# Moving the normalisation of a block into the next round, the masks ahead of the variance, and the key turns behind half a step

## What is computed

```
S_t = S_{t-1} diag(w_t) - (S_{t-1} kk_t)(kk_t*a_t)^T + v_t k_t^T ;  y_t = S_t r_t
mean = mean(y); var = mean(square(y - mean))          # over the 64 columns of a head
yn = (y - mean) * rsqrt(var + GN_EPS)
out = (yn * gn_w + gn_b + bonus) * g
```

## Time and profile before

| | |
|---|---|
| median of three runs | 1400.87 us (1399.13 to 1403.6) |
| profiled execution, its own time | 1397.37 us |
| span in that profile | 1395.7 us |
| PE busy | 1304.2 us, 93% |
| DVE / ACT / POOL busy | 635.5 / 470.3 / 250.8 us |
| the four rounds | about 192 to 355 us of the span |
| behind them to the second half of the output product | 355 to 386 us |

### The profile page before, as it was taken

How to read it: one execution, slowest core, us unless ns; L and a number is a source line. 1 busy time by engine, 2 the same in 40 slices (tenths; PEclk the granted TensorE clock), 3 DMA queues, 4 the chain that set the end, 5 groups by cost and what they waited for, 6 DMA issues and landing times.

```text
span 1395.7 us, 25137 instructions
## 1 busy us (share of the span) xinstructions
PE 1304.2 (93%) x10577; PEld 1163.4 (83%) x10577; DVE 635.5 (46%) x763; ACT 470.3 (34%) x758; POOL 250.8 (18%) x228
## 2 busy tenths in 40 slices
PE   5999989888799999999999887987999999999998
PEld 5677878777699889988899876865998899988998
DVE  5578635454347552134422646265255432245323
ACT  4446435335245222222222431266232211222222
POOL 6013325232102220012211030110003200022000
PEclk9999999999899999999999998998999999999999
DMA  5223100001052322223242122100313322222321
GB/s 181 75 61 120 61 2 3 2 3 50 14 182 75 107 91 95 90 91 104 72 151 92 61 68 91 61 1 19 118 61 104 106 91 91 90 90 90 106 92 61
DMA packets 99929, 108.95 MB, mean 78 GB/s; under 512 B 1907, under 2 KB 97189, under 8 KB 99845
## 3 DMA queue, kind: packets, MB, share of 16 engines
q1 hardware_dynamic: 99764, 107.45, 23.9%
q0 software_dynamic: 80, 0.26, 0.1%
HBM read 105.60 MB, written 2.10 MB: 77 GB/s over the span
## 4 chain that ended last, share of the span: by engine, by line
PE 78%; DVE 9%; issue 5%; ACT 4%; POOL 2%; DVEq 2%; POOLq 1%; ACTq 0%; DMA 0%
PE ps L404 11%; PE ps L406 11%; PE ps L405 11%; PE ps L439 10%; PE ps L440 10%; PE ps L441 10%; DVE w_lo L1420 2%; PE ps L490 1%; PE ps L491 1%; PE ps L492 1%; PE ps L432 1%; PE ps L430 1%; PE ps L431 1%; DVE rcnt L1911 1%; PE ps L668 1%
## 5 line engine op out<-in xcount | busy, mean ns | idle before, releaser
L1420 DVE TENSOR_TENSOR w_lo<-w_raw,w_hi 128x2048 fp32r<-128x2048 f32 (+1 forms) x93 | 212.1, 2280 | 241.4 <-ACT w_hi L985 238.2
L439 PE MATMUL ps<-w_hi,a_hi 128*128 128x256 f32 x1024 | 288.4, 282 | 0.9 <-DVE w_lo L1420 0.9
L440 PE MATMUL ps<-w_lo,a_hi 128*128 128x256 f32 x1024 | 288.0, 281 | 0.0
L441 PE MATMUL ps<-w_hi,a_lo 128*128 128x256 f32 x1024 | 288.0, 281 | 0.0
L404 PE MATMUL ps<-h_hi,w_hi 128*128 128x512 f32 x672 | 270.9, 403 | 13.1 <-DVE w_lo L1420 12.8
L406 PE MATMUL ps<-h_hi,w_lo 128*128 128x512 f32 x672 | 266.1, 396 | 0.0
L405 PE MATMUL ps<-h_lo,w_hi 128*128 128x512 f32 x672 | 266.0, 396 | 0.0
L985 ACT ACTIVATE w_hi<-w_raw 128x2048 fp32r<-128x2048 f32 (+1 forms) x90 | 171.2, 1903 | 162.8 <-PE ps L441 141.1
L2141 POOL TENSOR_TENSOR hsq<-tmp 128x512 f32<-128x512 f32 x64 | 103.3, 1616 | 568.3 <-ACT tmp L989 568.3
L439 PEld LDWEIGHTS ps<-w_hi,a_hi 128*128 128x128 f32 x1024 | 193.2, 189 | 1.5 <-DVE w_lo L1420 1.3
L440 PEld LDWEIGHTS ps<-w_lo,a_hi 128*128 128x128 f32 x1024 | 193.2, 189 | 0.2
(11 more groups left out here) (316 smaller groups left out, 1845.8 us busy)
## 6 DMA issues: line engine op xcount, KB each, us to landing
w_raw<-w_ffn_up_dram SPq DMA_DIRECT2D x16, 1024.0 KB, 5.3
w_raw<-w_ffn_down_dram SPq DMA_DIRECT2D x16, 1024.0 KB, 5.0
w_raw<-w_up_dram SPq DMA_DIRECT2D x16, 1024.0 KB, 5.3
w_raw<-w_down_dram SPq DMA_DIRECT2D x16, 1024.0 KB, 4.9
w_raw<-w_in_first_dram SPq DMA_DIRECT2D x12, 1024.0 KB, 5.3
w_raw<-w_out_dram SPq DMA_DIRECT2D x8, 1024.0 KB, 5.9
w_raw<-w_in_dram SPq DMA_DIRECT2D x8, 1024.0 KB, 5.3
xn<-x_dram SPq DMA_DIRECT2D x8, 512.0 KB, 6.5
```

The source lines that it names most:

```text
L439: mm(o, hi[:, hb + k, tok], whi, start=first and own and k == ks[0], stop=False, skip_group_check=True)
L440: mm(o, hi[:, hb + k, tok], wlo, start=False, stop=False, skip_group_check=True)
L441: m = mm(o, lo[:, hb + k, tok], whi, start=False, stop=last and k == ks[-1], skip_group_check=True)
L1420: v.tensor_tensor(w_lo[:, g % 2, :, 0:n], w_raw[:, g % 2, :, 0:n], w_hi[:, g % 2, :, 0:n].bitcast(F32), ALU.subtract).then_inc(sm["w_lo_re ...
```

## The change

- PE: `turn_keys(i)` leaves `beside(i, 9)` and comes behind the second `attend` of the last step, still with its waits for `v_ready` and `kap_ready` (in the last round for `yc_ready` alone). The last round's `turn_output(2)` goes to bank 7, and `out_part(3)`, which writes bank 7, gets a wait for `y_scaled`.
- ACT: `turned_keys(i)` (the two evacuations) comes behind the second `attend` too. The squares carry a scale of 64^-0.5. Behind the last block's outputs ACT takes the square root of its variance.
- DVE: `variance(i-1)` moves from n = 7, where it stood before the masks of LA, to n = 8, behind them and before the masks of KA. `normalised(i-1)` leaves n = 8 and comes at n = 1 of the next round (as `normalised(i-2)`); only in the last round it stays at n = 8. For the last block DVE takes the reciprocal of ACT's root. The variance's second instruction only adds.
- POOL: `root` of the last block is gone.

```diff
@@ PE, beside(i, n)
                 if n == 9 and i + 1 < NB:
                     pe.wait_ge(sm["ka_masked"], 2 * i + 4)
                     turn_values(i + 1)
-                    pe.wait_ge(sm["v_ready"], i + 2)
-                    pe.wait_ge(sm["kap_ready"], i + 2)
-                    turn_keys(i)
                 if n == 9 and i + 1 == NB:
-                    pe.wait_ge(sm["yc_ready"], i)
-                    turn_output(i - 1, 2)
-                    pe.wait_ge(sm["y_scaled"], i)
-                    turn_keys(i)
+                    turn_output(i - 1, 7)
@@ PE, rounds
                     attend(m + 1)
+                if i + 1 < NB:
+                    pe.wait_ge(sm["v_ready"], i + 2)
+                    pe.wait_ge(sm["kap_ready"], i + 2)
+                else:
+                    pe.wait_ge(sm["yc_ready"], i)
+                turn_keys(i)
@@ PE, behind the rounds
             out_part(2, 0, HP)
+            pe.wait_ge(sm["y_scaled"], NB - 1)
             out_part(3, 0, HP)
@@ ACT
-                af(ysq[:, :, :], yc[:, :, :], ACT.Square).then_inc(sm["ysq_ready"], 1)
+                af(ysq[:, :, :], yc[:, :, :], ACT.Square, scale=N ** -0.5).then_inc(sm["ysq_ready"], 1)
...
-                if n == 9:
-                    turned_keys(i)
...
+                turned_keys(i)
...
             output(NB - 1, 2)
+            act.wait_ge(sm["var_ready"], NB)
+            af(yrs[:, :], var[:, :], ACT.Sqrt).then_inc(sm["yrs_ready"], 1)
@@ DVE
-                v.tensor_scalar(var[:, :], var[:, :], 1.0 / N, GN_EPS, ALU.mult, ALU.add).then_inc(sm["var_ready"], 1)
+                v.tensor_scalar(var[:, :], var[:, :], GN_EPS, None, ALU.add).then_inc(sm["var_ready"], 1)
...
                 dve.wait_ge(sm["yrs_ready"], i + 1)
+                if i + 1 == NB:
+                    v.reciprocal(yrs[:, :], yrs[:, :])
+                    dve.drain()
...
-                if n == 7 and i:
-                    variance(i - 1)
+                if n == 1 and i > 1:
+                    normalised(i - 2)
                 if n == 7 and i + 1 < NB:
                     masked(i + 1, LA, "la_done", "la_masked")
                 if n == 8 and i:
+                    variance(i - 1)
+                if n == 8 and i + 1 == NB:
                     normalised(i - 1)
...
                 if n == 9 and i + 1 == NB:
-                    scaled_output(i - 1, 2)
+                    scaled_output(i - 1, 7)
@@ POOL, behind the rounds
             shifted_output(NB - 2)
-            root(NB - 1)
             shifted_output(NB - 1)
```

## The result

The changed kernel took 1380.65 us (median of four runs, 1380.14 to 1381.18) against 1400.82 (1399.13 to 1403.6) for the kernel before: ratio 0.986, interval 0.9843 to 0.9878. Over all jobs of this study (67 timed runs of the kernel before, median 1399.6, 1397.0 to 1405.0; 13 of the changed one, median 1381.2, 1380.1 to 1383.3) it is 18.5 us. The 67 leave out x1's twelve runs of the kernel before, which would not move their median by more than 0.1. Executions that lie far off are left out of every figure here: two of the kernel before of 1842 us at a mean granted clock of 0.65, one of 4454 us in x2 and one of 6408 us in x4. The two profiled executions took 1397.37 and 1380.14 us: 17.2 apart.

A forecast was written before the change was run, and what follows sets the result against it. The rounds were taken as bound by PE's order, with DVE's program, waiting for POOL's root, releasing their ends. Gains 7.55 + 4.1 + 0.3 + 1.6 = 13.55, say 13.5 us, off 1400.87 gave 1387.4 us; range 1382 to 1393.5.

The forecast's parts named there:

- turn 1 to 2: Passage from round 1 to 2: scores 0.8, PE's gap 3.5, clock 2.4, key turns 0.85; 7.55 us won.
- the clock's 2.4: Turn from round 1 to 2: half clock behind PE's gap goes, 2.4 us won, bounds 0 to 3.4.
- the key turns' 1.65: Key turns behind the second attend no longer wait for ACT's copies: 0.3, 0.85 and 0.5 us in the three turns.
- turn 2 to 3: Passage from round 2 to 3: scores 0.8, gap 2.77, keys 0.5; 4.1 us won, bounds 3 to 4.5.
- the tail's root: Last block's root moves from POOL to ACT; multiply some 0.9 us earlier but hidden by out_part(3), gain 0.
- the last solve's start: Last round: key turns directly follow turn_output, no longer waiting for bank 2; 1.6 us won, bounds 0.5 and 4.5.
- rival B: Last round gets its clock back, key turns and solve faster: 15.8 us won, 1385.1 us; chance 0.12.
- so I take the difference off the median: Whole kernel: profiled execution lies 3.5 us below the median, so the 13.5 us come off 1400.87, giving 1387.4.
- A: Rounds: the half clock only moves elsewhere, so the 2.4 is not won: 11.1 us won, 1389.8; chance 0.15.
- C: Turns: ACT becomes the bound, key copies behind a waiting exponential; 2.2 us lost, 11.3 won, 1389.6; chance 0.13.
- D: Half clock from the last round's larger gap lasts up to 380 us: 18 us more, 1405.4, slower; chance 0.03.
- E: Rounds: POOL keeps masks or first levels late, the 3.5 gap stays; about 5 us won, 1395.9; chance 0.05.

The follow-up runs named there:

- x1: The kernel before, unchanged, profiled and timed again: 1399.75 us median, single runs 1397.56 to 1403.76.
- x2: The kernel before with only the key turns and their ACT evacuations moved behind each round's second attend: 1399.41 us against 1399.04, ratio 0.9998.
- x4: The changed kernel with the last round's part undone (turn_output through bank 2, key turns behind y_scaled): 1388.29 us.
- x6: The changed kernel with twelve small DVE multiplies ahead of the masks of KA in round 1, putting a gap back: 1392.02 us.
- x3: The kernel before with only DVE's two moves in the rounds (variance, normalising): 1388.98 us, ratio 0.9922.
- x8: The changed kernel with the last block's root back on POOL, without DVE's reciprocal: 1381.26 us, ratio 0.9871.
- x5: The kernel before with 14 extra PE matmuls ahead of the last round's turn_output(2): 1398.22 us against 1400.45, ratio 0.9978.
- x9: The changed kernel itself, profiled and timed again: 1382.96 us (1381.98 to 1383.25).
- x13: The changed kernel with 22 extra PE matmuls behind the last turn of the output: 1381.73 us.
- x14: The changed kernel with x13's 22 fillers and block 2's output turned only behind the last solve: 1380.75 us.
- x15: The changed kernel with nine extra PE matmuls (2.05 us) behind the last solve: 1385.07 us.
- x16: The changed kernel with 18 extra PE matmuls (4.1 us) behind the last solve: 1386.61 us.

## Why the prediction was wrong

**Right.** What bound the rounds (DVE's wait for the root, handed on to PE at their ends); turn 1 to 2 with its four terms (7.75 against 7.55: 4.4 against 4.3 for scores and gap, 3.4 against 3.25 for clock and keys), the clock's 2.4 among them (2.3 by x6); the key turns' 1.65 in all, in the stage once the gaps are gone (1.7 in x4 against x3), though not in the total time (0.7 there, nothing in x2); turn 2 to 3 (4.6 against 4.1: the first double follows the keys at once, and `key_values` waited for no copy); turn 0 to 1 (0.3); the moved multiply at nothing (0.65 us under DVE's wait for the next half copy); the tail's root at nothing (x8); the last solve's start (2.1 against 1.6: the key turns at full clock took 0.9 less, and the inverse, named as late next, then bound it).

**Wrong, first step.** "The solve itself stays at the half clock: 3.68 us". It took 1.96. The forecast took the larger gap before `turn_output` as the reason for the half clock and gave the other outcome (rival B) 0.12. x4 has the gap and, behind it, the wait of 2.9 us, and falls to half clock; the changed kernel has the same gap without that wait, and doesn't; x5 fills both and doesn't. The solve took 3.3 to 3.7 us in all five profiles with bank 2 and no filler (the kernel before, x1 to x4), and 1.96 or 1.97 in x5 and in all fourteen with the edit. So it is the edit in the last round that gave the solve its clock back: 2.0 us in the two profiles behind the start of the solve, 2.7 between x4 and the changed kernel. Why x6 had half clock for the turns just ahead of the solve, and the other profiles with the edit had not, stays open.

**Wrong, second step.** "so I take the difference off the median". That holds only if both medians lie as far above their profiled executions, and they lay 3.5 and 0.5 us above them. Of the 20.2 us, 2.9 are this; over all jobs, with medians of 1399.6 and 1381.2, the difference of 18.5 is only 1.3 above that of the profiles. That the change took away stretches which the first profile lacked is not shown: by x1 those lie at the entry of round 0 and behind the stage, where nothing was changed, and x9 has the first of them in the changed kernel too. So most of the 2.9 is the luck of which executions four runs drew. The range took 2 us for scatter and held it to be the same on both sides. With x9's job (1382.96) the result would have been inside; so it would with either of the two steps put right by itself (2.0 or 2.9 us on 1380.65, against the range's 1382).

**The rivals.** A (the half clock only moves) fails in the rounds and is seen elsewhere: x2, x13 and x14. B came. C: the exponential does stand before the key copies, and nothing waited for them. D and E did not come; in no profile did the half clock last from the last round to the last turn of the output.

**Open.** Where half clock falls in the stages behind 380 us, and why it is stable within most jobs and differs between them. The experiments ran on five chips, one for each job, so a difference between chips is a rival that no run here excludes; x9's three slower runs and its faster one, on one chip, show that it can't be all of it. x15 and x16 don't decide whether it depends on the time of arrival.

## What to carry to other kernels

A root computed by another engine should not stand in front of masks that the critical engine waits for: issue the multiply one round later, where its engine waits anyhow. When TensorE's waits are removed at several places, count the half clock behind each and ask what is left between one wait and the next; a freed PSUM bank was worth some 2.2 us of waits and 3.6 of clock up to the end of its stage (x4: 5.8 in all, of which 2.7 lie behind the solve's start and 0.9 in the key turns). Before a difference is added to a median, look at the scatter of the times: a spread of 4 us, with a clock that mostly moves along with it, says that the profile shows one draw of several.

## What was not expected of the hardware

- Gaps of 2.77 and 2.78 us at the same place were followed by a granted clock of 1.00 in one kernel and 0.66 over the next 5 us in another (before and x2). The same happens within one kernel: behind a wait of 1.4 us at the entry of round 0 the next step took 3.23 us in the first profile of the kernel before and 4.87 in x1. The length of the gap alone doesn't tell.
- Keeping TensorE busy with useless matmuls for 3.4 us made a kernel 2.2 us faster (x5); at a second place it kept the clock at 1.00 there and won nothing in total (x13, x14).
- A 128x128 float32 matmul of the fillers shows as two instructions of 0.11 us each (44 of them: 88, 9.99 us), so a filler costs twice its count.
